# A hybrid decoder step: cached pages laid out for the chip by the host code, page scores in four column groups

## The reference, cut to what matters

```
h = rms(x) ; z = h @ w_in                       # 1024 -> 8800 columns, split by purpose
A: HGRN2 gated recurrence over chunks of 64, state 4 x 128 x 128 per sequence
B: DSA: indexer scores pick the top 256 of 1024 past keys (64 of 256 for the prompt),
   then softmax attention over the picked keys
C: NSA: attention over compressed blocks (32 tokens, stride 16, a small MLP:
   silu(blk @ w1 + b1) @ w2), over the best 64-token blocks, and over the last 512 tokens
out = (sum of sigmoid-gated branch projections) @ w_out + x
```

## Time and profile before

| | |
|---|---|
| time, median of 3 runs | 1076.0 us (1073.6 to 1079.0) |
| the profiled execution | 1082.4 us, span 1080.7 us |
| busy: PE, PEld, DVE, ACT, POOL | 96%, 79%, 55%, 39%, 18% of the span |
| mean granted clock of TensorE | 0.983 of full speed |
| DMA | 189.2 MB, mean 175 GB/s |

### The profile page before, as it was taken

The page is one execution under the profiler, slowest core; times in us unless marked ns, Lnnn a source line. Parts: engine busy times, 40 slices in busy tenths (PEclk is TensorE's granted clock), DMA queues, the critical chain, the costliest instruction groups (busy, mean ns, idle before and its releaser), DMA issues.

```text
span 1080.7 us, 20490 instructions
## 1 busy us (share of the span) xinstructions
PE 1040.3 (96%) x7392; PEld 849.4 (79%) x7392; DVE 590.6 (55%) x1596; ACT 422.4 (39%) x869; POOL 199.3 (18%) x356
## 2 busy tenths in 40 slices
PE   8999999999999999999999999999999999999999
PEld 6888678867777777888888886798667777777887
DVE  4133488876567874224240346887865678722241
ACT  2136332256524774220021544322673457723100
POOL 0300130020214447000030003100203334550000
PEclk9999999999999999999999999999998999999999
DMA  6633367243374789734443433763433768895342
GB/s 243 207 131 127 98 226 265 94 142 119 130 270 126 239 269 260 232 131 152 155 156 128 155 127 79 294 193 111 157 118 109 254 179 252 266 268 190 117 156 79
DMA packets 93895, 189.22 MB, mean 175 GB/s; under 512 B 19650, under 2 KB 70226, under 8 KB 82018
## 3 DMA queue, kind: packets, MB, share of 16 engines
q1 hardware_dynamic: 78530, 138.63, 38.9%
q0 software_dynamic: 14976, 49.03, 14.4%
q10 hardware_dynamic: 288, 0.24, 0.1%
HBM read 177.60 MB, written 18.63 MB: 182 GB/s over the span
## 4 chain that ended last, share of the span: by engine, by line
PE 79%; DVE 10%; ACT 4%; issue 3%; DVEq 3%; DMA 1%; ACTq 0%; SPq 0%
PE ps L914 21%; PE ps L1051 16%; PE ps L1411 8%; PE ps L1419 5%; PE ps L1286 4%; PE ps L903 3%; PE ps L1298 3%; PE ps L1079 2%; PE ps L1256 2%; DVE arena L2217 2%; DVE arena L2226 1%; PE ps L1191 1%; PE ps L1179 1%; PE ps L1382 1%; DVE top L1910 1%
## 5 line engine op out<-in xcount | busy, mean ns | idle before, releaser
L914 PE MATMUL ps<-hT,slab 128*128 128x264 f32 (+1 forms) x1152 | 263.7, 387 | 0.0
L1431 ACT ACTIVATE arena<-ps 64x256 f32<-64x256 f32 (+17 forms) x350 | 184.4, 547 | 183.9 <-PE ps L914 70.4
L914 PEld LDWEIGHTS ps<-hT,slab 128*128 128x128 f32 (+1 forms) x1152 | 216.4, 190 | 38.5 <-issue 2.7
L1051 PE MATMUL ps<-hT,slab 128*128 128x264 f32 x768 | 187.8, 403 | 0.0
L1051 PEld LDWEIGHTS ps<-hT,slab 128*128 128x128 f32 x768 | 149.6, 199 | 32.3 <-DVEq L2131 3.2
L613 POOL DMA_DIRECT2D arena<-in_cache_kv_dram x64 | 34.6, 540 | 344.8 <-PE ps L992 197.6
L1411 PE MATMUL ps<-Y,slab 128*128 128x264 f32 x384 | 85.8, 386 | 0.0
L1411 PEld LDWEIGHTS ps<-Y,slab 128*128 128x128 f32 x384 | 73.0, 190 | 12.5
L1298 PE MATMUL ps<-arena,w 128*128 128x128 f32 x512 | 69.5, 280 | 7.5 <-ACT arena L1431 4.1
L1861 DVE SCALAR_TENSOR_TENSOR arena<-arena,small 128x264 f32<-128x264 f32 x26 | 11.0, 489 | 114.9 <-ACT arena L1511 114.9
L1298 PEld LDWEIGHTS ps<-arena,w 128*128 128x128 f32 x512 | 61.8, 191 | 12.7 <-DVE arena L2226 5.9
(11 more groups left out here) (370 smaller groups left out, 1421.7 us busy)
## 6 DMA issues: line engine op xcount, KB each, us to landing
slab<-in_weights_dram SPq DMA_DIRECT2D x84, 1024.0 KB, 5.0
arena<-in_cache_kv_dram POOLq DMA_DIRECT2D x64, 192.0 KB, 3.9
arena<-in_cache_kv_dram SPq DMA_DIRECT2D x64, 192.0 KB, 4.0
arena<-in_cache_kv_dram POOLq DMA_DIRECT2D x64, 128.0 KB, 6.6
arena<-in_cache_kv_dram SPq DMA_DIRECT2D x64, 128.0 KB, 6.8
out_dram<-in_state_win_dram POOLq DMA_DIRECT2D x2, 4088.0 KB, 26.2
slab<-in_weights_dram SPq DMA_DIRECT2D x8, 512.0 KB, 6.1
arena<-in_state_hgrn_dram SPq DMA_DIRECT2D x8, 512.0 KB, 11.3
```

Source lines behind the costliest of these rows:

```text
L914: last = mm(ps[0:job[3], n % 2, 0:LT], v[:, k, job[2]:job[2] + job[3]], hT[:, k, :], start=(k == 0), stop=(k == KD - 1))
L1051: last = mm(ps[:, bank, 0:LT], v[:, k, (d % 2) * 128:(d % 2) * 128 + 128], hT[:, k, :], start=(k == 0), stop=(k == KD - 1))
L1431: return A(out, in_, ACT.Copy, scale=scale)
```

## The change

`kernel()` lays out the cache, the windows and the states in memory in another order before the launch. A page becomes three blocks: `keys` (128 partitions x 512 floats: compression k and v already in the pair layout that the MLP's first matrix takes, then dsa keys and selection keys with channels on the partitions), `vals` (128 x 256) and `index` (64 x 128). Window keys come with channels first. On the chip all transposes of them go, with the copies behind them, and so do the spread queries, "qr" and the pads. The page stage has 8 units of 8 pages: half of the pages of two sequences, p and p + 4. Page scores are matmuls of 128 rows and 32 output columns; the four of a unit (dsa or selection, sequence p or p + 4) write to the four quarters of the output partitions. The compression runs both k heads or v heads of a pair with a block-diagonal `w2`. Keys have four buffers of one unit each, and all index keys have a buffer of their own. New rows leave the chip as they stand in `Z`, and the host code puts the rows together; only the values are still transposed (9 transposes). The first slab arrives in quarters.

```diff
-STREAM.insert(STREAM.index("m21"), "qr")
-PADS = ("pad0", "pad1")
-for _n, _next in zip(PADS, ("m03", "m12")):
-    STREAM.insert(STREAM.index(_next), _n)
...
-    ("n3", [(C_NWK, 256)], [("T", Z_NWK, 0, 128), ("V", "win", 128, 128, 128)]),
+    ("n3", [(C_NWK, 256)], [("T", Z_NWK, 0, 128), ("T", Z_NWV, 128, 128)]),
...
+            cuts = (0, n // 4, n // 2, n) if name == "iq0" else (0, n)
+            return [(dst[:, i:j], src[:, i:j]) for i, j in zip(cuts, cuts[1:])]
+        def queries_of(a, s):
+            o = s * (ROWS + NH) - s % NPAIR * NH
+            return QC[:, a, o:o + 32]
...
         def load_index_keys(engine, l, pair, pages):
-            u = pair % 2
-            engine.wait_ge(skey_p.sem, skey_p(l, f"T {pair - 2}") if pair >= 2 else skey_p.before(l, f"T {pair + 2}"))
...
+        def load_keys(engine, l, u, odd, pages):
+            if u >= 4:
+                engine.wait_ge(pg_p.sem, pg_p(l, f"u {u - 4}"))
+            for e in range(2):
+                for k in (odd, 2 + odd):
+                    engine.dma_start(KB[u % 4][:, e, k, :], page_of("keys", l, pages[u // 2 + NPAIR * e, 4 * (u % 2) + k])).then_inc(page_in[u % 4][odd], 16)
...
+                load_keys(sp, l, 0, 0, pages)
+                load_keys(sp, l, 1, 0, pages)
+                load_values(sp, l, 0, 0, pages)
+                sp.wait_ge(spill_out, l * 16 + 16)
                 window_keys(sp, l, 0)
+                window_keys(sp, l, 1)
                 for name in ("m13", "m20"):
                     send(name)
                 sp.wait_ge(cp_p.sem, cp_p(l, "s"))
+                load_keys(sp, l, 2, 0, pages)
                 load_values(sp, l, 1, 0, pages)
-                load_keys(sp, l, 1, 0, pages)
                 sp.wait_ge(cp_v.sem, cp_v(l, "sums"))
+                load_keys(sp, l, 3, 0, pages)
+                load_values(sp, l, 2, 0, pages)
+                for name in ("m21", "m22"):
+                    send(name)
+                for u in range(4, NUNIT):
+                    load_keys(sp, l, u, 0, pages)
+                    if u % 2:
+                        window_keys(sp, l, u // 2)
+                sp.wait_ge(pg_p.sem, pg_p(l, "u 4"))
+                for s in (4, 5):
                     load_values(sp, l, s, 0, pages)
...
-                    for z, r, o, b in ((Z_DK, 128, 0, 0), (Z_DV, 128, 128, 0), (Z_IK, HD, 256, 0), (Z_NCK, 128, 320, 0),
-                                       (Z_NCV, 128, 0, 1), (Z_NSK, 128, 128, 1), (Z_NSV, 128, 256, 1), (Z_NWK, 128, 384, 1)):
-                        last = nc.tensor.transpose(ps[0:n, 2 + 2 * t + b, o:o + r], Z[0:r, z, cols], ident[0:r, 0:r])
+                    for i, z in enumerate((Z_DV, Z_NSV, Z_NWV)):
+                        last = nc.tensor.transpose(ps[0:n, 2 + t, 128 * i:128 * i + 128], Z[:, z, cols], ident)
...
-                    copy(row[0:n, t, 0:448], ps[0:n, b, 0:448])
-                    copy(row[0:n, t, 448:832], ps[0:n, b + 1, 0:384])
-                    copy(wrow[0:n, t, 0:128], ps[0:n, b + 1, 384:512])
+                    copy(vrow[0:n, t, :], ps[0:n, 2 + t, 0:384])
...
+                def page_scores(u):
+                    p, hf = u // 2, u % 2
+                    for a, o in enumerate((K_DSA, K_SEL)):
+                        for e in range(2):
+                            mm(ps[quarter[2 * a + e], hf, :].rearrange("p (i t) -> p i t", i=4), queries_of(a, p + NPAIR * e), KB[u % 4][:, e, :, o:o + PAGE],
+                               start=(p == 0), stop=(p == NPAIR - 1))
+                def window_scores(p):
+                    pe.wait_ge(win_in[p % 2], (l * 2 + p // 2 + 1) * 32)
+                    for th in range(2):
+                        for e in range(2):
+                            mm(ps[quarter[2 * th + e], 2, 0:256], queries_of(1, p + NPAIR * e), kws[p % 2][:, e, 256 * th:256 * th + 256],
+                               start=(p == 0), stop=(p == NPAIR - 1))
+                def compress(u):
...
+                    for kv in range(2):
+                        for t in range(ST):
+                            o = K_CMP + (kv * ST + t) * 2 * NPB8
+                            last = mm(out[:, kv, :, 64 * hf:64 * hf + 64], w1[:, kv, t, :], blocks[:, :, o:o + 2 * NPB8],
+                                      start=(t == 0), stop=(t == ST - 1))
...
+                for u in range(NUNIT):
+                    for i in range(2):
+                        pe.wait_ge(page_in[u % 4][i], (l * 2 + u // 4 + 1) * 64)
...
+                    page_scores(u)
+                    if u % 2:
+                        window_scores(u // 2)
+                    compress(u)
+                    if u >= 2 and u % 2 == 0:
+                        compressed(u // 2 - 1)
```

More of the change, by code:

```diff
@@ L838, in _ @@
[L838 to L845 removed]
+                pool.wait_ge(mx_a.sem, mx_a(l, "m 7"))
+                if l:
+                    pool.wait_ge(back_in, l * 16)
```

648 lines of the change are left out of this document (235 added, 413 removed).

## The result

| | before | after |
|---|---|---|
| median of the runs, us | 1077.52 (1073.55 to 1081.29, 4 runs) | 1007.2 (1004.78 to 1011.44, 4 runs) |
| profiled run: time, span | 1082.4, 1080.7 | 1005.99, 1004.3 |
| ratio | | 0.9352, 95% interval 0.9303 to 0.9401 |

The forecast was 995 us with 975 to 1040 as its range; 1007.2 us lies inside it, 12.2 us above the forecast. The kernel is faster by 6.5%: 70.3 us between the medians, 76.4 us between the two profiled spans.

The account below looks back on a forecast made before the run. TensorE, busy 96% of the span, was taken as the bound. 2 x (1.8 + 3.0 + 0.5 + 4.1 + 30.8) + 1 = 81.4 us off 1082.4, less 6.4 for the median, gave 995 us, range 975 to 1040.

Parts of the forecast that it names:

- waits of over 5 us for a unit: Page stage: a sign that, if seen in the profile after, would make the forecast wrong.
- the part forecast at 0.5: Compression of the prompt's blocks: two matmuls for four, 0.5 us less per layer.
- The page stage: Eight units scoring and compressing pages: 47.5 us for 78.3, counted as 30.8 us less per layer.
- PE waits 1 to 2 us before each of units 5 to 7: Page stage: TensorE waits this long for late key loads, with unit 7 done at 386 us.
- the single line of 14.7 MB: Page stage: all loads from "sums" to unit 7 in one line, taking 41.1 us at 358 GB/s.
- the clock falls in the DMA-paced units: Rival, page stage: four units run at the lower clock, 10 us per layer, 1015 us; chance 0.13.
- Rows and index keys: New rows and index keys ahead of the search: fewer transposes shorten VectorE's chain, 3.0 us per layer (bounds 4.6 and 1.7).
- The branch gates: 325.44 to 342.67 us: 20 page transposes and a wait of 0.87 us go, 4.1 us less per layer.
- rivals on column groups: Page and window scores: column groups of 512 columns do not overlap, 21.3 us per layer, 1037 us; chance 0.10.
- runs of 16 floats: Rival, page stage: short runs of the moving operand halve compression's rate, 28 us per layer, 1051 us; chance 0.05.
- The start: First slab at 8.55 us: TensorE waits for a quarter instead of a half, 1 us less, once (0 to 2.5).
- Window values: Window values as a normal projection: 16 instructions of 264 columns replace those of L926 and L933, 1.8 us less per layer.

Follow-up runs that it names:

- Experiments 1: Kernel after, with SyncE issuing slabs m21 and m22 behind the key loads of units 4 to 7 instead of ahead of unit 4: 998.91 us.
- experiment 2: Kernel after, with SyncE issuing slabs m21 and m22 between the keys of unit 4 and unit 5: 1010.35 us.
- experiment 3: Kernel after, with SyncE issuing slabs m21 and m22 early, ahead of its wait for "sums": 996.55 us.
- 12: experiment 11 with SyncE's halves of the values of sequences 4 and 5 also held until unit 6 is done: 991.11 us.
- experiment 4: Kernel after, with 22 products of zeros added on TensorE just ahead of its wait for unit 4: 1010.78 us.
- experiment 8: Kernel after, with the 4 MB window-state copy issued only behind the first value product of the prompt attention (about 250 us): 1008.68 us.
- (5): Kernel after, with all four page-score products of a unit in one column group, scores not added over the pairs: 1030.39 us.
- experiment 11: Kernel after with slabs early, mix 16 wait behind first page scores, and GpSimd's values (sequences 4, 5) and window values held until unit 6 is done: 990.92 us.
- experiment 7: Kernel after, with the 4 MB window-state copy issued only behind the last index-key product (144.6 us): 1018.2 us.

## Why the forecast was right, and where it missed

The forecast was right in its number and in most of its parts: TensorE stayed the bound, the transposes' time came off, the column groups overlapped. It was not right in how the DMA meets TensorE in the page stage. The prediction's own list of signs against it had "waits of over 5 us for a unit", and 5.58 and 7.27 us came. That the stage still gave 28.7 us of the 30.8 forecast is in part luck: the time went into one long wait and a slow unit (7.3 us) instead of three short waits (3.7 us), and TensorE's own work was 1.5 us less. In all 12.2 us were missing. They are these:

- *The median.* The forecast took 6.4 us off the sum because the profiled run before lay that far above its median. The profiled run after lay 1.2 us below its own. The sum itself was 81.4 us and measured 76.4, so 5 us are the sum's. The rest, 7 to 8 us, is that the gain was read in a run that was slower than usual: between the medians it is 70.3. Part of it can be pointed to: 16 instructions of L1051 at 293.66 took 6.63 us, their successors at 287.26 took 5.49, for 3.8 at full clock, so over a microsecond of "gain" in the part forecast at 0.5 (2.2 measured) is clock.
- *The page stage: 28.7 (and 26.7) us for 30.8.* TensorE's own work was forecast at 43.8 us and is 42.3. The rate was forecast at 358 GB/s and was 382 to 408 from 340 to 370 us. Both were on the safe side. What failed is the step "PE waits 1 to 2 us before each of units 5 to 7", and with it the single line of 14.7 MB that it was worked out from. By that line 7.4 MB had to come up to unit 4, which makes 20.5 us and 2 to land: unit 4 at 360.2 with TensorE there at 360.0, 21.5 us after the stage's start, and no wait. In fact two lines load side by side, and the slabs stand in SyncE's alone. SyncE's has 4.7 MB up to its half of unit 4 (keys of unit 3, values, two slabs, keys of unit 4); at half of 385 GB/s, an estimate from the measured rate, they take 24.5 us from 330.95, and 2 to land make 357.5. Measured are 358.6, 26.3 us after the start, and TensorE is there after 20.8. GpSimd's line, without slabs, is far ahead by then. So one wait of 5.58 or 7.27 us came instead of three short ones; units 5 to 7 came in time. Experiments 1 to 3 show the part of the slabs: with the slabs gone from that place the long wait goes, with the slabs behind unit 4 it stands at unit 5; in 12 the stage of layer 0 runs at TensorE's pace. That it is the share between the queues rests on the landings; no run moved slabs or window keys to GpSimd's queue.
- *The rival "the clock falls in the DMA-paced units"* happened in one unit of eight, at 1.76 and 2.66 us, not in four at 10 (experiment 4). What the Trainium skill says in "TensorE: Matmul & The Clock Gate", section HAM oscillation, of products that start cold behind a DMA wait is what this trace shows behind the waits of 5.58 and 7.27 us: in 355 to 360 us the granted clock is 0.56. Behind one of 1.44 us in experiment 3 the page scores took 1.06 us, full speed.
- *Rows and index keys: 2.2 (layer 0), 3.1 (layer 1) for 3.0.* The step that followed VectorE's chain instead of TensorE's sum was right in layer 1, where L1020 is released by VectorE. In layer 0 the forecast had "released by VectorE" too, but the chain runs over the wait for index pages and TensorE; experiment 8 puts that at 1.3 us at L1007, which is more than what layer 0 lacks against layer 1 (0.9).
- *The branch gates: 2.4 for 4.1.* Here I let a wait of 0.87 us for VectorE go with the transposes; it is still there, 0.86 at 319.07, since it stands behind the first burst of the gates and has another cause than the pages. And the wait for mix 16, 0.57 us, came out from behind the page transposes that had hidden it.
- *No wait for a DMA at the value product* and none at unit 3 came, as forecast.
- *The rivals on column groups and on runs of 16 floats.* A burst is 1.06 us, and 3.59 without the groups (5). 32 compressing instructions take 3.84 us, 0.12 each as in the earlier trace rows: short runs of the moving operand cost nothing here.
- *The start: 1.5 for 1. Window values: 2.1 for 1.8.* As forecast.

Left open: where in the stage the hold of experiment 11 gives its 4 to 7 us, since its one profile shows 0.6 of them, and how the waits go when the two queues carry equal bytes. A wait at unit 4 filled for exactly its length was not tried.

## What to carry to other kernels

When a stage goes from engine-bound to nearly DMA-bound, put down for each buffer what is queued ahead of it, for each queue by itself, and compare it with the time at which the engine gets there; a total in MB over a rate gives the end of the stage but not the waits. Bulk that is needed later belongs where the DMA is idle, ahead of a wait that the issuing engine is about to enter (here 2 MB moved by a few lines, 10.7 us; values held back, 7 more by the medians, 4 to 5 at one clock). Idle time of TensorE that lies beside another chain is worth little: taking its cause away can move it, and the slow clock that follows it, onto the path.

## What was not expected of the hardware

- The idle pieces of 4 to 8 us looked at here cost TensorE 1.4 to 2.7 us more behind them (L1021 3.44 us for 2.05, unit 4 7.33 and 8.23 for 5.57), at a granted clock of 0.50 to 0.78. Shorter ones go either way: in experiment 11 unit 4 took 5.57 us behind a wait of 2.04 us in layer 0 and 7.18 behind one of 2.07 us in layer 1.
- The clock can differ between runs of the same instructions: the 16 of L992 at about 319 us, behind a wait of 0.86, took 3.8 us or so in the kernel after, 5.25 in experiment 4 and 6.89 in experiment 11. Such places may make up much of the spread of 2 to 15 us between runs of one kernel; only one run of each has a trace.
- Four column groups gave a factor of 3.53/1.00 = 3.5 on products of 32 stationary columns and 512 moving ones, two groups 1.8 by the forecast's row.
- A copy of 4 MB from HBM to HBM, 27.8 us long, made TensorE wait 4 us for index loads of 32 KB where it ran beside them (issued at 118.95, landed 21.87 us later), and 2.5 us for a weight slab in experiment 7.
- Loads issued together on two queues did not land together: SyncE's half of unit 4 came 7.7 and 9.4 us after GpSimd's, and in experiment 2 its half of unit 5 came 13.1 us after.
